# Rewritten step orders of an attention half, norm roots spread by transposes, and one softmax scaling fewer, in a two-layer encoder kernel

## The reference

```python
h = _rms(x, attn_norm[l]);  z = h @ w_in[l]
# four differential heads: q, k with two 64-wide parts, rope on both
p = softmax(sc);  a = p[:, :, 0] - lam * p[:, :, 1];  o = a @ v
o = _rms(o, subln_g) * (1.0 - lam_init)
# four latent heads: c_q, c_kv -> rms -> w_q_b, w_kv_b; scores = q_nope k_nope + q_pe k_pe
p = softmax(sc);  y = p @ v
x = x + concatenate([y_diff, y_mla]) @ w_o[l]
h = _rms(x, ffn_norm[l]);  x = x + (silu(h @ w_gate[l]) * (h @ w_up[l])) @ w_down[l]
```

## Time and profile before

| engine | busy us (share) | instructions |
|---|---|---|
| TensorE, matmuls | 2467.9 (93%) | 11236 |
| TensorE, weight loads | 2016.8 (76%) | 11236 |
| VectorE | 1365.7 (52%) | 2453 |
| ScalarE | 567.7 (21%) | 1089 |
| GpSimd | 937.2 (35%) | 798 |

### The profile page before, as it was taken

How to read it: one execution, slowest core, us unless ns; L and a number is a source line. 1 busy time by engine, 2 the same in 40 slices (tenths; PEclk the granted TensorE clock), 3 DMA queues, 4 the chain that set the end, 5 groups by cost and what they waited for, 6 DMA issues and landing times. The chain is left out here.

```text
span 2644.6 us, 30875 instructions
## 1 busy us (share of the span) xinstructions
PE 2467.9 (93%) x11236; PEld 2016.8 (76%) x11236; DVE 1365.7 (52%) x2453; ACT 567.7 (21%) x1089; POOL 937.2 (35%) x798
## 2 busy tenths in 40 slices
PE   5887899798999999999999899989899999999996
PEld 4766787676888888888887678767688888888885
DVE  4887658765333333333358853986633333333335
ACT  2334223441000010000124331444210000000001
POOL 6432400017666666665110010001544444444421
PEclk9989999998999999999999899999899999999998
DMA  7440442032333333332132125222211111111101
GB/s 259 146 142 24 177 165 96 32 128 96 120 119 120 122 123 119 119 121 70 71 116 87 69 80 182 89 80 80 96 48 48 48 48 48 48 50 53 48 24 64
DMA packets 50342, 249.49 MB, mean 94 GB/s; under 512 B 5968, under 2 KB 6096, under 8 KB 32720
## 3 DMA queue, kind: packets, MB, share of 16 engines
q1 hardware_dynamic: 49536, 247.52, 27.4%
q10 hardware_dynamic: 720, 0.86, 0.1%
HBM read 187.54 MB, written 60.82 MB: 94 GB/s over the span
## 5 line engine op out<-in xcount | busy, mean ns | idle before, releaser
L445 PE MATMUL bank<-h_hi,w 128*128 128x512 f32 x1792 | 708.7, 395 | 2.5 <-POOL w L575 1.7
L446 PE MATMUL bank<-h_lo,w 128*128 128x512 f32 x1792 | 700.3, 391 | 0.0
L447 PE MATMUL bank<-h_hi,w 128*128 128x512 f32 x1792 | 700.2, 391 | 0.0
L570 POOL TENSOR_TENSOR w<-raw,zero 128x512 fp32r<-128x512 f32 x318 | 338.7, 1086 | 870.5 <-PE bank L447 753.9
L575 POOL TENSOR_TENSOR w<-raw,w 128x512 fp32r<-128x512 f32 x318 | 416.9, 1332 | 12.5
L445 PEld LDWEIGHTS bank<-h_hi,w 128*128 128x128 f32 x1792 | 338.6, 189 | 80.0 <-issue 8.1
L446 PEld LDWEIGHTS bank<-h_lo,w 128*128 128x128 f32 x1792 | 338.6, 189 | 72.4 <-issue 2.9
L447 PEld LDWEIGHTS bank<-h_hi,w 128*128 128x128 f32 x1792 | 338.1, 189 | 71.5
L1375 DVE TENSOR_TENSOR x<-x,bank 128x512 f32<-128x512 f32 x352 | 239.9, 687 | 187.1 <-PE bank L447 184.1
L595 POOL TENSOR_TENSOR acc<-sq,zero 128x512 f32<-128x512 f32 x6 | 6.2, 1041 | 768.7 <-ACT sq L948 768.7
L445 PE MATMUL bank<-u_hi,w 128*128 128x512 f32 x704 | 273.9, 389 | 0.0
(11 more groups left out here) (165 smaller groups left out, 3487.6 us busy)
## 6 DMA issues: line engine op xcount, KB each, us to landing
w<-parked SPq DMA_DIRECT2D x81, 1024.0 KB, 4.8
raw<-in_wffn SPq DMA_DIRECT2D x132, 512.0 KB, 3.5
parked<-w SPq DMA_DIRECT2D x27, 1024.0 KB, 6.5
parked<-p SPq DMA_DIRECT2D x27, 1024.0 KB, 4.8
raw<-in_watt SPq DMA_DIRECT2D x27, 512.0 KB, 4.4
praw<-in_watt SPq DMA_DIRECT2D x27, 512.0 KB, 5.7
out_yT<-y_out SPq DMA_DIRECT2D x16, 256.0 KB, 2.2
x<-in_xT SPq DMA_DIRECT2D x4, 512.0 KB, 6.7
```

Of the source, the lines that this page charges most:

```text
L445: nc.tensor.matmul(out_ap, lhs[0], rhs[0], start=first, stop=False)
L446: nc.tensor.matmul(out_ap, lhs[0], rhs[1], start=False, stop=False)
L447: return nc.tensor.matmul(out_ap, lhs[1], rhs[0], start=False, stop=last)
L570: last = nc.gpsimd.tensor_tensor(w[slot][0][:, cols], src[:, cols], zeros_like(src[:, cols]), ALU.add)
```

## The change

Three things. The three lists are new, with the same steps, and GpSimd's work of the first half has a list too (`GPSIMD_ORDER`): the additions of squares lie between the splits of chunks 19 to 24. Where the old lists implied that a buffer was free, explicit waits are added: in ScalarE's rope and plain copies, latent copies and latent outputs, in VectorE's combine, in TensorE's first score unit of a head.

A spread is four transposes of one column of the root, read 128 times over, in place of a diagonal and a matmul. So the diagonal on VectorE goes, and the last of the 12 tiny operations releases TensorE.

In the differential combine the first probability isn't scaled. The second is scaled by -lam times the ratio of the sums, so a head's output is larger by the first sum; the norm behind it takes that away, with an epsilon multiplied by the square of the sum (one more tiny operation in RQ of y0 to y3).

```diff
-    V | P q0 | P k0 | P q1 | S 0 | Pa k1 | S 1 | Pb k1 | T 0 | S 2 | Pa q2 | T 1 | Pb q2 | A 0 | S 3 | T 2 | S 4 |
-    Pa k2 | T 3 | S 5 | Pb k2 | A 1 | T 4 | Pa q3 | S 6 | ST y0 | T 5 | S 7 | RB y0 | Pb q3 | A 2 | T 6 | S 8 |
-    Pa k3 | T 7 | S 9 | Pb k3 | A 3 | T 8 | S 10 | ST y1 | P ckv | T 9 | S 11 | RB y1 | P kpe | A 4 | T 10 | S 12 |
-    ST ckv | P cq0 | T 11 | S 13 | RB ckv | P cq1 | A 5 | T 12 | S 14 | P kn0 | ST cq | T 13 | S 15 | RB cq | A 6 |
-    T 14 | P pe0 | P qn0 | P pe1 | T 15 | S 16 | ST y2 | A 7 | P vm0 | P vm1 | S 17 | RB y2 | P vm2 | T 16 | S 18 |
-    P vm3 | ST y3 | P kn1 | P qn1 | T 17 | S 19 | RB y3 | A 8 | T 18 | S 20 | P oa0 | T 19 | S 21 | A 9 | P oa1 |
-    T 20 | S 22 | P kn2 | P qn2 | T 21 | S 23 | T 22 | S 24 | P kn3 | P qn3 | T 23 | A 10 | S 25 | ST n | A 11 |
-    S 26 | P oa2 | T 24 | RB n | P oa3 | T 25 | S 27 | A 12 | P oa4 | T 26 | S 28 | P oa5 | T 27 | S 29 | A 13 |
-    T 28 | S 30 | T 29 | P oa6 | S 31 | A 14 | T 30 | P oa7 | T 31 | Pa ob0 | A 15 | Pa ob1 | Pb ob0 | Pb ob1 |
-    P ob2 | P ob3 | P ob4 | P ob5 | P ob6 | P ob7
+    V | P q0 | P k0 | P q1 | S 0 | Pa k1 | S 1 | Pb k1 | T 0 | S 2 | Pa q2 | S 3 | T 1 | Pb q2 | Pa k2 | S 4 | T 2 |
+    A 0 | S 5 | Pb k2 | T 3 | Pa q3 | A 1 | S 6 | T 4 | Pb q3 | ST y0 | S 7 | T 5 | P k3 | S 8 | T 6 | Pa kpe | A 2 |
+    S 9 | Pb kpe | T 7 | RB y0 | Pa ckv | S 10 | A 3 | T 8 | S 11 | Pb ckv | T 9 | ST y1 | S 12 | T 10 | Pa cq0 |
+    RB y1 | S 13 | Pa cq1 | ST ckv | T 11 | Pb cq0 | S 14 | RB ckv | Pb cq1 | S 15 | ST cq | A 4 | T 12 | RB cq |
+    T 13 | A 5 | T 14 | P kn0 | P pe0 | P qn0 | T 15 | ST y2 | A 6 | A 7 | S 16 | P vm0 | S 17 | P vm1 | RB y2 |
+    P vm2 | S 18 | P vm3 | T 16 | P kn1 | ST y3 | P qn1 | S 19 | P kn2 | RB y3 | S 20 | P pe1 | S 21 | T 17 | S 22 |
+    P qn2 | T 18 | A 8 | S 23 | P kn3 | P oa0 | T 19 | P qn3 | T 20 | A 9 | S 24 | S 25 | S 26 | S 27 | T 21 | P oa1 |
+    S 28 | T 22 | P oa2 | T 23 | A 10 | S 29 | T 24 | S 30 | A 11 | T 25 | P oa3 | T 26 | P oa4 | T 27 | S 31 | A 12 |
+    T 28 | A 13 | ST n | T 29 | P oa5 | T 30 | P oa6 | T 31 | A 14 | A 15 | P oa7 | P ob0 | P ob1 | P ob2 | RB n |
+    P ob3 | P ob4 | P ob5 | P ob6 | P ob7
-    V | RH q0 | RH k0 | EX 0 | RH q1 | EX 1 | TH 0 | EX 2 | TH 1 | RH k1 | EX 3 | TH 2 | EX 4 | TH 3 | RH q2 | TH 4
-    | EX 5 | YC 0 | EX 6 | TH 5 | RH k2 | EX 7 | TH 6 | SH y0 | EX 8 | TH 7 | RH q3 | EX 9 | YC 1 | TH 8 | EX 10 |
-    TH 9 | RH k3 | EX 11 | TH 10 | SH y1 | LC ckv | EX 12 | TH 11 | EX 13 | RH kpe | YC 2 | TH 12 | SH ckv | LC cq0
-    | LC cq1 | EX 14 | TH 13 | PH kn0 | EX 15 | TH 14 | SH cq | PH qn0 | RH pe0 | TH 15 | RH pe1 | PH vm0 | EX 16 |
-    PH vm1 | EX 17 | YC 3 | TH 16 | SH y2 | PH vm2 | PH vm3 | EX 18 | TH 17 | PH kn1 | PH qn1 | EX 19 | TH 18 |
-    SH y3 | EX 20 | TH 19 | EX 21 | SQ 0 | SQ 1 | YC 4 | TH 20 | SQ 2 | SQ 3 | EX 22 | TH 21 | PH kn2 | PH qn2 |
-    SQ 4 | EX 23 | TH 22 | SQ 5 | SQ 6 | SQ 7 | EX 24 | TH 23 | PH kn3 | PH qn3 | EX 25 | YC 5 | TH 24 | EX 26 |
-    TH 25 | EX 27 | TH 26 | EX 28 | TH 27 | EX 29 | YC 6 | TH 28 | EX 30 | TH 29 | EX 31 | TH 30 | TH 31 | SN 0 |
-    SN 1 | YC 7 | SN 2 | SN 3 | SN 4 | SN 5 | SN 6 | SN 7
+    V | RH q0 | RH k0 | EX 0 | EX 1 | RH q1 | TH 0 | EX 2 | TH 1 | RH k1 | EX 3 | TH 2 | EX 4 | RH q2 | EX 5 | TH 3 |
+    YC 0 | TH 4 | RH k2 | EX 6 | RH q3 | TH 5 | EX 7 | TH 6 | EX 8 | RH k3 | TH 7 | EX 9 | EX 10 | SH y0 | TH 8 |
+    YC 1 | TH 9 | EX 11 | LC ckv | TH 10 | EX 12 | RH kpe | SH y1 | TH 11 | EX 13 | EX 14 | SH ckv | LC cq0 | LC cq1 |
+    TH 12 | EX 15 | TH 13 | SH cq | YC 2 | PH kn0 | TH 14 | PH qn0 | TH 15 | RH pe0 | EX 16 | PH vm0 | PH vm1 |
+    PH vm2 | YC 3 | PH vm3 | PH kn1 | SH y2 | EX 17 | TH 16 | PH qn1 | EX 18 | EX 19 | SQ 0 | PH kn2 | SQ 1 | TH 17 |
+    SH y3 | EX 20 | SQ 2 | TH 18 | PH qn2 | RH pe1 | PH kn3 | EX 21 | TH 19 | PH qn3 | EX 22 | EX 23 | EX 24 | TH 20 |
+    YC 4 | EX 25 | EX 26 | TH 21 | TH 22 | EX 27 | TH 23 | TH 24 | SQ 3 | SQ 4 | YC 5 | TH 25 | EX 28 | TH 26 |
+    EX 29 | EX 30 | SQ 5 | SQ 6 | TH 27 | SQ 7 | SN 0 | TH 28 | SN 1 | SN 2 | TH 29 | EX 31 | SN 3 | SN 4 | SN 5 |
+    TH 30 | YC 6 | TH 31 | YC 7 | SN 6 | SN 7
-    V | RP q0 | RL q0 | RP k0 | RL k0 | MX 0 | RP q1 | CB 0 | MX 1 | RL q1 | CB 1 | TL 0 | MX 2 | RP k1 | TL 1 |
-    CB 2 | MX 3 | RL k1 | TL 2 | CB 3 | MX 4 | RP q2 | TL 3 | CB 4 | MX 5 | RL q2 | TL 4 | CB 5 | MX 6 | RQ y0 |
-    RP k2 | CB 6 | TL 5 | MX 7 | AP y0 | RL k2 | CB 7 | TL 6 | MX 8 | AL y0 | RP q3 | TL 7 | CB 8 | MX 9 | RL q3 |
-    TL 8 | CB 9 | MX 10 | RQ y1 | RP k3 | TL 9 | AP y1 | MX 11 | RL k3 | CB 10 | TL 10 | CB 11 | MX 12 | AL y1 |
-    RQ ckv | RP kpe | AP ckv | CB 12 | MX 13 | TL 11 | RL kpe | TL 12 | AL ckv | CB 13 | MX 14 | RQ cq | TL 13 |
-    CB 14 | MX 15 | PL kn0 | AP cq | AL cq | TL 14 | CB 15 | RP pe0 | PL qn0 | RL pe0 | TL 15 | MX 16 | RP pe1 |
-    RQ y2 | PL vm0 | PL vm1 | CB 16 | MX 17 | RL pe1 | AP y2 | PL vm2 | TL 16 | PL vm3 | CB 17 | MX 18 | AL y2 |
-    RQ y3 | TL 17 | CB 18 | MX 19 | PL kn1 | PL qn1 | AP y3 | TL 18 | AL y3 | CB 19 | MX 20 | TL 19 | CB 20 | XO oa0
-    | MX 21 | TL 20 | XO oa1 | CB 21 | MX 22 | TL 21 | CB 22 | MX 23 | PL kn2 | YL 4 | PL qn2 | TL 22 | CB 23 |
-    MX 24 | TL 23 | CB 24 | MX 25 | PL kn3 | PL qn3 | RQ n | CB 25 | MX 26 | XO oa2 | YL 5 | TL 24 | CR n | TL 25 | CB 26 |
-    MX 27 | XO oa3 | XO oa4 | TL 26 | MX 28 | CB 27 | TL 27 | CB 28 | MX 29 | XO oa5 | TL 28 | CB 29 | MX 30 | YL 6
-    | XO oa6 | TL 29 | CB 30 | MX 31 | CB 31 | TL 30 | XO oa7 | TL 31 | LN 0 | YL 7 |
-    LN 1 | XO ob0 | LN 2 | XO ob1 | LN 3 | LN 4 | XO ob2 | LN 5 | XO ob3 | LN 6 | LN 7 |
-    XO ob4 | XO ob5 | XO ob6 | XO ob7
+    V | RP q0 | RL q0 | RP k0 | RL k0 | RP q1 | MX 0 | MX 1 | CB 0 | CB 1 | RL q1 | MX 2 | TL 0 | RP k1 | CB 2 |
+    RL k1 | MX 3 | TL 1 | RP q2 | MX 4 | TL 2 | CB 3 | MX 5 | CB 4 | CB 5 | TL 3 | RL q2 | RP k2 | MX 6 | RL k2 |
+    TL 4 | RP q3 | RQ y0 | MX 7 | TL 5 | CB 6 | RL q3 | MX 8 | CB 7 | TL 6 | RP k3 | MX 9 | RL k3 | CB 8 | TL 7 |
+    RP kpe | MX 10 | AP y0 | CB 9 | CB 10 | TL 8 | AL y0 | MX 11 | TL 9 | RQ y1 | MX 12 | CB 11 | TL 10 | AP y1 |
+    MX 13 | CB 12 | AL y1 | RQ ckv | CB 13 | MX 14 | AP ckv | RL kpe | TL 11 | CB 14 | MX 15 | AL ckv | RQ cq |
+    TL 12 | AP cq | TL 13 | AL cq | CB 15 | PL kn0 | TL 14 | RP pe0 | PL qn0 | TL 15 | RL pe0 | MX 16 | RQ y2 |
+    PL vm0 | CB 16 | PL vm1 | MX 17 | PL vm2 | AP y2 | MX 18 | PL vm3 | PL kn1 | RQ y3 | PL qn1 | CB 17 | MX 19 |
+    CB 18 | AP y3 | TL 16 | MX 20 | PL kn2 | TL 17 | AL y2 | RP pe1 | PL qn2 | AL y3 | TL 18 | MX 21 | MX 22 | CB 19 |
+    PL kn3 | CB 20 | TL 19 | RL pe1 | MX 23 | MX 24 | CB 21 | XO oa0 | TL 20 | MX 25 | PL qn3 | MX 26 | CB 22 |
+    TL 21 | YL 4 | XO oa1 | CB 23 | TL 22 | MX 27 | CB 24 | MX 28 | TL 23 | MX 29 | CB 25 | TL 24 | CB 26 | XO oa2 |
+    MX 30 | TL 25 | CB 27 | XO oa3 | TL 26 | CB 28 | YL 5 | TL 27 | LN 0 | CB 29 | TL 28 | MX 31 | CB 30 | XO oa4 |
+    TL 29 | LN 1 | LN 2 | CB 31 | TL 30 | YL 6 | XO oa5 | TL 31 | LN 3 | LN 4 | XO oa6 | YL 7 | LN 5 | LN 6 | XO oa7 |
+    XO ob0 | RQ n | XO ob1 | XO ob2 | LN 7 | XO ob3 | CR n | XO ob4 | XO ob5 | XO ob6 | XO ob7
+""")
+
+GPSIMD_ORDER = order("""
+    W 0 | W 1 | W 2 | W 3 | W 4 | W 5 | W 6 | W 7 | W 8 | W 9 | W 10 | W 11 | W 12 | W 13 | W 14 | W 15 | W 16 |
+    W 17 | W 18 | W 19 | AD 0 | AD 1 | AD 2 | W 20 | W 21 | W 22 | AD 3 | AD 4 | W 23 | AD 5 | AD 6 | AD 7 | W 24 |
+    W 25 | W 26
...
-RSQRT_LINKS = 12
+RSQRT_LINKS = 11
...
+LAST_Z = max(TILE[n] for n in TILES if n[0] in "qk" and n[1].isdigit() or n in ("kpe", "ckv", "cq0", "cq1"))
-PRE_DVE = PRE_LAM + 4 * L
+PRE_DVE = PRE_LAM + 3 * L
-FINAL_DG = FINAL_ADD + RSQRT_LINKS + 1
+FINAL_COLUMN = FINAL_ADD + RSQRT_LINKS + 1
...
-        s_dg = Count(sem("rstd_diagonal"), NSTAT, layer=NSTAT_LAYER, before=1)
+        s_dg = Count(sem("rstd_made"), NSTAT, layer=NSTAT_LAYER, before=1)
...
-        LINKS_HALF = (NSTAT - 1) * RSQRT_LINKS + NORM_LINKS + 3 * 16 + 16
+        LINKS_HALF = (NSTAT - 1) * RSQRT_LINKS + NORM_LINKS + H + 2 * 16 + 16
...
+            def add_square(which, l, b, k):
+                pool.wait_ge(s_sq.sem, f(s_sq, sq_at + k))
+                if k == 0:
+                    pool.wait_ge(s_st.sem, f(s_st, st0 - 1))
+                    nc.gpsimd.tensor_tensor(acc[:], sq[0][:], zero[:].to_broadcast([P, T]), ALU.add).then_inc(s_add.sem, 1)
+                else:
+                    pool.wait_ge(s_add.sem, f(s_add, add0 + k - 1))
+                    nc.gpsimd.tensor_tensor(acc[:], acc[:], sq[k % 2][:], ALU.add).then_inc(s_add.sem, 1)
+            def add_squares(which, l, b=0):
+                    add_square(which, l, b, k)
...
-            for j in range(NCH):
+            for kind, j in GPSIMD_ORDER:
+                if kind == "AD":
+                    add_square("tail", 0, 0, j)
+                    continue
-                if CHUNKS[j] == "oa0":
-                    add_squares("tail", 0, 0)
...
-            def spread(wait, done):
+            def spread(wait, done, column, at):
```

(77 more changed lines are left out.)

15 lines of the change are left out of this document (3 added, 12 removed).

## The result

The changed kernel takes 2514.43 us (2510.22 to 2515.04, four runs), the kernel before in the same session 2645.82. The ratio is 0.950, 95% interval 0.948 to 0.952. It is 131 us faster; the forecast was 2542, so the direction held and the size was short by 28 us.

A forecast was written before the change was run, and what follows sets the result against it. TensorE was taken as the bound, other engines counting only where it waits. Savings of 61.5 (waits), 23 (clock), 11.5 (spreads) and 5.4 (outside the halves) made 101 off 2644.6: span 2543, forecast 2542 us, range 2512 to 2588.

The forecast's parts named there:

- Waits: TensorE's idle time in the four attention halves falls from 101.5 to 40 us, saving 61.5.
- say 5, with what I don't see 8 a half: TensorE waits left per half under the new order: 5 us for named places, 8 with unseen ones.
- Clock: TensorE's time at the lower clock in the halves falls from 85 to 30 us, saving 23; bounds 0 and 40.
- Spreads: 28 spreads in the halves, transposes replacing the matmul, save 0.41 us each: 11.5; bounds 0 and 21.
- The scaling and the diagonal: VectorE loses 11.8 us a half, hidden behind TensorE; without that the orders' margin would fall below zero.
- Outside the halves: Cheaper spreads, dropped diagonals and two memsets outside the halves, including the serial program end, save 5.4 us.
- Added waits: The explicit waits added on ScalarE, VectorE and TensorE, and GpSimd's and SP's order, cost 0.
- rival F: Slower: a ring of TensorE and ScalarE waits around the exponentials closes; 2671 us at 1 us a unit, chance 0.03.
- tally of loads: TensorE's summed work against VectorE's up to A 9: the new order has a reserve of 8.6 us a half.
- rival C: Waits come back elsewhere because the tally leaves out latency; 57 us gained, 2587 us, chance 0.15.
- TensorE must wait at least 6 us by load alone, and every dependent chain adds to it, because there is no reserve: Old order up to A 9: TensorE 140 us, VectorE 140.5, which starts 5.5 us in.
- rival B: Nothing left to wait for: idle 20 instead of 40, clock saving 33; 131 us gained, 2513 us, chance 0.14.

The follow-up runs named there:

- gp_memset: Changed kernel with GpSimd's weight splits in the first half writing zeros as low halves instead of subtracting; 2483.47 us.
- diag: Changed kernel with the spread made by the diagonal and one matmul again; 2537.44 us.
- orders_only: Changed kernel's new orders, with the diagonal and matmul spread again and one extra pass over `e` in each differential combine; 2547.72 us.
- cq_near: Changed kernel with the sums and spread of cq moved directly before their first use, no load changed; 2537.53 us.
- scale1: Changed kernel with one extra pass over `e` (factor 1) in each differential combine; 2521.87 us.
- old_orders: Changed kernel with the three old lists and GpSimd's additions where they were; transposed spreads and dropped scaling stay; 2623.05 us.
- scale3: Changed kernel with three extra passes over `e` (factor 1) in each differential combine; 2590.55 us.
- old_cq_far: Changed kernel with the three old lists, and in them the sums and spread of cq moved earlier; 2640.52 us.

## Why the prediction came out as it did

The forecast was 101 us less of span; it was 132.

1. **Waits (forecast 61.5, measured 74).** Idle time in the halves fell from 101.5 to 27.3. The step that failed in size is "say 5, with what I don't see 8 a half": of the three places that I named, the spread of cq was 0.53 late (0.7 forecast), that of y2 0.9 (0.6), no wait stands at S 16 (1.5), and the 3 us for the unseen were not there. The first half kept 20.4, not 16, and gp_memset, where 6.4 are left, shows what is in it: in the main VectorE stopped by GpSimd. All of the changed kernel's waits over 2 us in the halves are there. The kvb wait went as said.
2. **Clock (23, about 29).** About 82 us at the half level (85 by the rounded clocks) became 24, all in the first half; half of the 58 between is 29. I left 30, spread over all halves, because waits of about 1 us were to stay. The clock did not fall in halves whose longest wait was 0.9 us, nor in the second halves of diag and orders_only, where it was 1.6; in that of cq_near, with one of 2.5, 10 us ran at half clock.
3. **Spreads (11.5, 11; with step 5's and the diagonal 23).** diag has 0.40 a spread, as the rows of before said.
4. **The scaling and the diagonal ("hidden").** The scaling nearly is (scale1: 0.6 us in the second half, but 4.2 in the first). The diagonal is not where TensorE waits for the root: 1.8 us in diag's second half. The sentence that without the two the margin would fall "below zero" overrates the load: orders_only had just that load, and its idle time rose by 0.6 us apart from the waits for the diagonal.
5. **Outside the halves (5.4, 4).** 4.3 by the stretches.
6. **Added waits (0).** None appears; rival F is out.

These make 118 of the 132. The remaining 14 lie inside TensorE's busy time of the halves: it fell by 53.6 us (the earlier trace rows against the same rows after), clock and spreads explain 40. The runs tell where it comes from: with the half clock taken out, TensorE's busy time in the second half is 238.4 in old_orders (246.85, less half of 17 us) and 235.3 in the changed kernel, with the same operations. So about 3 us a half, 12 of the 14, come with the orders. What in the orders does it stays open. Products overlap in the records (one lasts 0.39 and the next starts after 0.23), so waits and handovers shorter than about 0.15 us stand in busy time, and fewer of them is my reading, which no run tested.

The reasoning that led to the sum was half right. The tally of loads gives the reserve of the new order within some 2 us (scale1, scale3) and was right against rival C. As the cause of the old waits ("TensorE must wait at least 6 us by load alone, and every dependent chain adds to it, because there is no reserve") it failed: old_orders had 10 us more reserve and 3 us less waiting, orders_only had none by the tally and waited 4.7. What fits these rows is the distance of each chain, the work that TensorE has between its start and its use: cq_near paid 23 us for taking that away from one. That every wait of the old order went for this reason is argued, not shown, and old_cq_far, where one distance grew and the kernel became slower, shows that a single distance is not the whole account. I had put the distances behind the loads, in one sentence, and gave rival B 0.14 because roots "remain serial"; they are serial in VectorE, but TensorE, in the halves without splits, now has work for all but 0.5 to 0.9 us of each. What was to stay was summed over named places by their distances, not by the loads; so the 28 us by which the sum was off say nothing for the account by load.

## What to carry to other kernels

For every dependent chain between in-order engines, count the other work that the waiting engine has between the step that starts the chain and the one that needs it, and compare that with the chain's length; the sums of load only say how much slack all chains have together. Move a step with its producers on every engine, or the wait turns up at the next of them. A removed wait can count twice, for itself and for the half clock behind it: here 74 us of waits took 29 us of clock loss with them.

## What of the hardware was unexpected

GpSimd's splits of the weights stretch VectorE's steps of 0.16 us to between 0.96 and 1.18 in the first half; with zeros written instead of a subtraction (537 ns, no tensor read, against 1390) the kernel is 31 us faster, 6 of them before the first product. A GpSimd instruction of one input takes 1556 ns where that of two takes 1123, and the kernel still gains 14 us by it; VectorE's two-input steps of 0.16 us mostly keep their length beside it.

A transpose of one column repeated 128 times costs what a transpose of a full tile does (four take 0.65 us, and 0.63 for `e`).
